# A hybrid decoder layer on one core: SBUF tiles filled up to multiples of 256 bytes, and attention's PSUM banks divided three and three

## The chip, the core and the metric

One core of a Trainium2 chip runs the whole layer as one program. The metric is the device time of one execution in microseconds (us), lower is better. Most executions of a kernel agree closely, but the three timed ones of the kernel before spread over 15 us. TensorE (PE) multiplies matrices, VectorE (DVE), ScalarE (ACT) and GpSimd (POOL) do the rest, SyncE (SP) issues most DMAs. SBUF is the on-chip working memory of 128 partitions, and PSUM, with eight banks of 2 KB in each partition, takes TensorE's results.

## The reference

A decoder layer over 1024 tokens of width 1024, all in float32:

```
h = x
proj = rmsnorm(h) @ w_in                      # queries, keys, values, gates of two groups of heads
o_nsa = gated sum of three attention branches # 8 heads: compressed, selected blocks, window of 512
o_fox = softmax attention with cumulative log-forget bias   # 8 heads
h = h + concat(rmsnorm(o_nsa), rmsnorm(o_fox)) @ w_out
u = rmsnorm(h)
h = h + hierarchical mixture of experts(u)    # 4 groups x 4 experts, top group, top 2 in it
h = h + sigmoid(rmsnorm(h) @ w_ple_gate + b) * (p @ w_ple_proj)
return rmsnorm(h)
```

An expert is `silu(u @ w_gate) * (u @ w_up) @ w_down` with an inner width of 512.

## The kernel before

The program is five stages, one behind the other, with a barrier of all engines between them where a `Scope` ends: projection (`stage_project`), attention (`stage_attention`), output mix (`stage_mix`), experts (`stage_moe`) and the final stage (`stage_finish`).

**Matmuls in three parts.** For nearly full float32 precision each wide product is made of three matmuls (`mm3`, lines 140 to 142): ScalarE rounds an operand to a "hi" tile (fp32r), VectorE or GpSimd takes the remainder into a "lo" tile, and TensorE adds hi x hi, hi x lo and lo x hi in PSUM. In the page's names a matmul reads "out<-streamed,stationary": the stationary tile (128 x 128) is loaded as weights (PEld), the streamed one passes with up to 512 columns. Projection streams `prj_hT` against `att_w_hi`/`att_w_lo`; the mix streams `mix_w` against `mix_mT`; the experts stream `exp_g_hi`/`exp_g_lo` (gate and up weights) against `moe_xT`, and `exp_d_hi`/`exp_d_lo` against `moe_hT`; the final stage streams the same `exp_g` tiles (with other weights in them) against `fin_vT`.

**Experts.** Tokens are sorted into tiles of 128 by expert, 21 tiles here for 16 experts. A tile takes 16 x 3 matmuls for gate and up (`gate_up`), 8 transposes of the next tile's tokens, 8 x 3 matmuls for the tile before (`down`) and 4 transposes. Where a tile begins a new expert, ScalarE (L2006, L2012) and VectorE (L2097, L2102) split its 12 chunks of weights, and SyncE loads the chunks of the expert behind it as soon as the raw buffers are read.

**Attention.** `units` are (head, branch, half of the queries): 64 of them, cut into 240 `banks`, each up to 512 score columns. TensorE's loop over banks b is, in this order: the scores of bank b+1 (L1334, L1347), some minima of the next head (`minimum`, L1303), the causal masks of bank b+1 (L1356), now and then the transposition of a head's minima (`turn`, L1313), and the weighing of bank b's values by its probabilities (`weigh`, L1374). ScalarE makes the exponentials (L1426). The scores are in two PSUM banks (`ps_s`, `ST`). Minima go through a ring of `MX` = 4 banks (`ps_m`): `place` counts the bank, `ring_before` names what must have been read before TensorE writes it, the minimum taken by VectorE (L1468, L1471; `min_taken`) or the rows copied by ScalarE (`min_copied`). The weighed sums of a unit go to one of two banks of `ps_o`: before the first weighing of unit u TensorE waits for `o_made` of unit u-2. VectorE's order is: the minima of bank b, then, if a unit has ended, its `leave` (L1495, L1499, L1502, L1506 or L1511), which divides the sums and signals `o_made` (behind L1511 by a semaphore instruction of its own, L1515). The blocks branch has one bank to a unit, the others three to seven.

The memory map of the program before has 16,512 bytes taken ahead of the kernel's first tile `all_c`, whose address is thus 16,512. The addresses of the tiles that the text speaks of, modulo 256:

| tiles | start modulo 256 |
|---|---|
| all_c (address 16,512) | 128 |
| att_o (address 25,856), att_cos, att_sin, att_w_out, att_w_raw, att_w_hi, att_w_lo, att_q_two0 | 0 |
| prj_hT_hi, prj_hT_lo | 128 |
| att_k_raw0, att_q_raw1, att_q_one1 and 2, att_q_two1 and 2, att_k_one1, att_k_two1, att_w_one1, att_w_two, att_x_one, att_x_two, att_prob, tok_kc_hi, tok_kc_lo | 192 |
| mix_w_hi, mix_w_lo | 0 |
| mix_mT_hi, mix_mT_lo, mix_x, mix_h, mix_u | 128 |
| exp_g_raw, exp_d_raw, exp_g_hi, exp_g_lo, exp_d_hi, exp_d_lo, exp_h | 0 |
| moe_xT_hi, moe_xT_lo, moe_hT_hi, moe_hT_lo, moe_y | 64 |
| fin_vT_hi, fin_vT_lo | 0 |

A 128-column slice is 512 bytes, so slices start at the same place modulo 256 as their tile. In attention the first buffer of several sets is a part of the projection's weight tiles (`held`): `att_w_hi` in a score row is q_one of every third head (or k_two), `att_w_lo` is k_one or w_one of the first group.

Of the kernel before, what the change touches and what calls it, by code (L numbers as in the profile page):

```python
# [29 lines left out]
F32 = mybir.dt.float32  # L30
F32R = mybir.dt.float32r
BF16 = mybir.dt.bfloat16
# [6 lines left out]
P = 128  # L39
# [41 lines left out]
HV = HD + 1  # L81
# [41 lines left out]
class Tally:  # L123

    def __init__(self, sem, base=0):
        self.sem, self.base, self.n = sem, base, 0
# [23 lines left out]

class Scope:

    def __init__(self, nc, name):
        self.nc, self.name, self.ctx, self.sems = nc, name, ExitStack(), []

    def __enter__(self):
        self.ctx.__enter__()
# [2 lines left out]
    def __exit__(self, *a):  # L162
        if self.sems:

            self.nc.all_engine_barrier()
            self.nc.clear_and_free_semaphores(self.sems)
            self.nc.all_engine_barrier()
        return self.ctx.__exit__(*a)

    def sb(self, name, shape, dt=F32):  # L170

        tile = self.ctx.enter_context(self.nc.sbuf_tensor(f"{self.name}_{name}", shape, dt))
        used = math.prod(shape[1:]) * (2 if dt is BF16 else 4)
        if 0 < used % 64 <= 32:
            self.ctx.enter_context(self.nc.sbuf_tensor(f"{self.name}_{name}_fill", [P, 8], F32))
        return tile

    def ps(self, name, shape, dt=F32):
        return self.ctx.enter_context(self.nc.psum_tensor(f"{self.name}_{name}", shape, dt))
# [8 lines left out]

def stage_project(nc, a, K, T):

# [7 lines left out]
    with Scope(nc, "prj") as sc:  # L198
# [5 lines left out]
        hT_lo = sc.sb("hT_lo", [P, KD, S], F32R)  # L204
        w_raw, w_hi, w_lo = (K[n] for n in ("w_raw", "w_hi", "w_lo"))

        k_raw0, q_raw0, q_one0, k_one0, k_two0, near0 = (t.rearrange("p k n -> p (k n)") for t in (
            w_raw[:, 0], w_raw[:, 1], w_hi[:, 1], w_lo[:, 1], w_hi[:, 0], w_lo[:, 0]))
        q_two0 = K["q_two0"][:]

        K["gf"] = K["o"][:, 4, 256:512].rearrange("p (t n) -> p t n", t=NT)
        K["kc_raw"] = K["o"][:, 4, 512:512 + GROUPS * P].rearrange("p (g n) -> p g n", g=GROUPS)
        mT0, mx0 = K["o"][0:3 * NT, 4, 768:768 + P].bitcast(F32R), K["o"][:, 4, 896:896 + NT * 5]

# [780 lines left out]
def stage_attention(nc, a, K, T):  # L995

    with Scope(nc, "att") as sc:
        HEADS = 2 * NH
        QS, RAW, ST, MX, PT, TM = 3, 2, 2, 4, 3, 2
        held = [K[n][:, s].rearrange("p k n -> p (k n)") for n in ("w_raw", "w_hi", "w_lo") for s in range(2)]  # L1000
        k_raw = [sc.sb("k_raw0", [P, S]), held[0]]
        q_raw = [held[1], sc.sb("q_raw1", [P, S])]
# [13 lines left out]
        tmp = sc.sb("tmp", [P, TM, 4, HD])  # L1016
        ps_s = sc.ps("ps_s", [P, ST, 512])
        ps_m = sc.ps("ps_m", [P, MX, 512])
        ps_o = sc.ps("ps_o", [P, 2, 512])

        q_in, k_in = [T["q_in0"], sc.sem("q_in1")], [T["k_in0"], T["k_in1"]]
        gk_hi, gk_lo, q_hi, q_lo, row_set, min_scored, min_taken, joined, min_turned, min_copied = (
# [18 lines left out]
        def pieces(b):  # L1041

            u, n = banks[b]
            out, at = [], 0
            for kb, qa, qb in BANKS[units[u][1]][units[u][2]][n]:
                out.append((kb, qa, qb, at))
                at += (qb - qa) * P
            return out, at
# [60 lines left out]
        with sc.block() as block:  # L1109
# [155 lines left out]
            def _(pe):  # L1265
                ident = c[:, K_ID:K_ID + P]

                def operands(i, br):

                    g, s = i // (NH // GROUPS), i % QS  # L1270
                    if br == CAUSAL:
                        return k_one[g], k_two[g], lambda kb: K["vsw"][:, kb, g, :]
                    if br == NEAR:
                        return w_one[g], w_two[g], lambda kb: K["vsw"][:, kb, GROUPS + g, :]
                    if br == BLOCKS:
                        return K["kc_hi"][:, g, :], K["kc_lo"][:, g, :], lambda kb: K["vc"][:, g, :]
                    f = i - NH
                    return fox_keys[f % QS][0], fox_keys[f % QS][1], lambda kb: K["vb"][:, kb, f, :]
# [82 lines left out]
                def weigh(b):  # L1361
                    u = banks[b][0]
                    i, br, half = units[u]
                    value = operands(i, br)[2]
                    first_of_unit = b == 0 or banks[b - 1][0] != u
                    pe.wait_ge(expd, b + 1)
                    if first_of_unit and u >= 2:
                        pe.wait_ge(o_made, u - 1)
                    first, final = first_of_unit, unit_end[u] == b + 1
                    parts = pieces(b)[0]  # L1370
                    for kb, qa, qb, at in parts:
                        for q in range(qa, qb):
                            end = final and (kb, q) == (parts[-1][0], qb - 1)
                            last = nc.tensor.matmul(ps_o[:, u % 2, (q % 4) * HV:(q % 4 + 1) * HV],  # L1374
                                                    prob[:, b % PT, at + (q - qa) * P:at + (q - qa + 1) * P], value(kb),
                                                    start=first, stop=end, skip_group_check=True)
                            first = False
                    last.then_inc(weighed, 1)
# [70 lines left out]
            def _(dve):  # L1449
# [38 lines left out]
                def leave(u):  # L1488
                    nonlocal parts
                    i, br, half = units[u]  # L1490
                    p = ps_o[:, u % 2, 0:4 * HV].rearrange("p (q d) -> p q d", q=4)
                    w = wt[:, u % 2, :]
                    qs = slice(4 * half, 4 * half + 4)
                    dve.wait_ge(weighed, unit_end[u])
                    own.inc(nc.vector.reciprocal(w, p[:, :, HD]))  # L1495
                    own.wait(dve)
                    if i < NH:
                        gate = i * 3 + (1 if br == CAUSAL else 2 if br == NEAR else 0)
                        own.inc(nc.vector.tensor_tensor(w, w, K["gate"][:, qs, gate], ALU.mult))  # L1499
                        own.wait(dve)  # L1500
                    if br == BLOCKS and half == 0:
                        own.inc(nc.vector.tensor_tensor(w[:, 0:1], w[:, 0:1], c[:, K_VALID:K_VALID + 1], ALU.mult))  # L1502
                        own.wait(dve)
                    wide = w.unsqueeze(2).to_broadcast((P, 4, HD))
                    if br in (CAUSAL, FOX):
                        nc.vector.tensor_tensor(K["o"][:, qs, i * HD:(i + 1) * HD], p[:, :, 0:HD], wide,  # L1506
                                                ALU.mult).then_inc(o_made, 1)
                        return
                    if parts >= TM:
                        dve.wait_ge(added, parts - TM + 1)  # L1510
                    own.inc(nc.vector.tensor_tensor(tmp[:, parts % TM], p[:, :, 0:HD], wide, ALU.mult))  # L1511
                    parts += 1
                    own.wait(dve)
                    dve.sem_inc(o_part, 1)
                    dve.sem_inc(o_made, 1)  # L1515

                first_keys(1, w_one[0], w_two[0])
                for b in range(NB):
# [4 lines left out]
                    if b and banks[b - 1][0] != banks[b][0]:  # L1523
                        leave(banks[b - 1][0])
                leave(banks[NB - 1][0])

# [1160 lines left out]
def build(nc, a, out):  # L2688
# [5 lines left out]
        "y": nc.dram_tensor("y_rows", [TILES * P, D], F32).ap(),  # L2694
    }
    K = {}
    with Scope(nc, "all") as outer:

        T["stored"] = [outer.sem(f"stored{i}") for i in range(2)]
# [58 lines left out]
```

## Time and profile before

| | us |
|---|---|
| median of the three timed executions | 1461.89 |
| the three | 1464.17, 1461.89, 1449.14 |
| the profiled execution, its own time | 1452.9 |
| its span in the trace | 1451.2 |
| its mean granted TensorE clock | 0.965 |

The profiled execution's own time is its span and 1.7 us around it. Stages by the trace, roughly: projection to 313, attention 314 to 714, mix to 853, routing and experts to 1300, final stage to 1451. TensorE's listed durations overlap, since matmuls are pipelined: the pace is read from starts.

### The profile page before, as it was taken

The page shows a single profiled execution, that of the slowest core. Times are in us where ns is not written, and L with a number is a line of the kernel's source. Part 1 is how long each engine was busy: PE and PEld are TensorE (multiplying, and loading weights), DVE is VectorE, ACT ScalarE, POOL GpSimd, SP SyncE. Part 2 cuts the span into 40 slices and gives each one's busy share as a digit, 9 for nine tenths or more (in the row PEclk, how much of TensorE's full clock was granted, in tenths as well). Part 3 has the DMA queues.
Part 4 walks back from the last instruction along what each step waited for, and adds up shares of the span by engine and source line. Part 5 has one row for each costly group of instructions (what it writes and reads, how often), then busy time and mean ns, then how long its engine had stood idle before and what let it go on. Part 6 is the DMA issues. An engine that isn't in the chain of part 4 may idle for free. (4 is left out here: it accounts for less than half of the span.)

```text
span 1451.2 us, 23331 instructions
## 1 busy us (share of the span) xinstructions
PE 1351.5 (93%) x7609; PEld 1133.5 (78%) x7610; DVE 773.9 (53%) x1575; ACT 619.8 (43%) x938; POOL 192.2 (13%) x219
## 2 busy tenths in 40 slices
PE   5899999989999999999889986999999999948996
PEld 4688888988888888888778864788888888837775
DVE  5734112646555554445353336678655767846762
ACT  5312111224333334444542213578644767845542
POOL 2100000115222123343000000000000000001100
PEclk9999999989999999999999977999999999969999
DMA  7233332122100111553232219699976979784411
GB/s 262 75 111 84 102 92 87 43 72 50 24 23 23 38 45 46 133 124 69 66 112 88 94 51 356 238 345 411 358 260 246 351 314 348 312 313 143 164 69 44
DMA packets 110994, 224.37 MB, mean 155 GB/s; under 512 B 17469, under 2 KB 44461, under 8 KB 110910
## 3 DMA queue, kind: packets, MB, share of 16 engines
q1 hardware_dynamic: 96694, 180.90, 36.7%
q0 software_dynamic: 10272, 30.57, 5.9%
q10 hardware_dynamic: 3944, 11.81, 2.2%
q8 instruction: 49, 0.80, 0.2%
q14 instruction: 35, 0.29, 0.1%
HBM read 178.66 MB, written 36.24 MB: 148 GB/s over the span
## 5 line engine op out<-in xcount | busy, mean ns | idle before, releaser
L1426 ACT ACTIVATE att_prob<-att_ps_s 128x512 f32<-128x512 f32 (+1 forms) x240 | 134.5, 561 | 240.0 <-PE att_ps_s L1356 200.0
L1471 DVE CUSTOM_DVE_ANT_0 att_ps_m<-att_ps_m,tok_maskb 128x128 f32<-128x128 f32 (+3 forms) x260 | 111.0, 474 | 140.7 <-PE att_ps_m L1303 137.7
L2097 DVE TENSOR_TENSOR exp_g_lo<-exp_g_raw,exp_g_hi 128x1024 fp32r<-128x1024 f32 x128 | 146.8, 1220 | 12.8 <-ACT exp_g_hi L2006 12.8
L1374 PE MATMUL att_ps_o<-tok_vsw,att_prob 128*128 128x65 f32 x1056 | 142.4, 277 | 0.8 <-DVEq L1515 0.5
L140 PE MATMUL moe_ps_g<-exp_g_hi,moe_xT_hi 128*128 128x512 f32 x336 | 136.2, 405 | 3.9 <-DVE exp_g_lo L2097 2.5
L1374 PEld LDWEIGHTS att_ps_o<-tok_vsw,att_prob 128*128 128x128 f32 x1056 | 134.5, 196 | 3.8 <-ACT att_prob L1426 1.0
L141 PE MATMUL moe_ps_g<-exp_g_lo,moe_xT_hi 128*128 128x512 f32 x336 | 134.4, 400 | 0.0
L142 PE MATMUL moe_ps_g<-exp_g_hi,moe_xT_lo 128*128 128x512 f32 x336 | 134.0, 399 | 0.0
L2006 ACT ACTIVATE exp_g_hi<-exp_g_raw 128x1024 fp32r<-128x1024 f32 x128 | 123.6, 1046 | 22.2 <-issue 11.5
L140 PE MATMUL prj_ps_w<-prj_hT_hi,att_w_hi 128*128 128x512 f32 x256 | 103.9, 406 | 5.4 <-ACT att_w_hi L492 2.1
L141 PE MATMUL prj_ps_w<-prj_hT_lo,att_w_hi 128*128 128x512 f32 x256 | 102.8, 402 | 0.0
L142 PE MATMUL prj_ps_w<-prj_hT_hi,att_w_lo 128*128 128x512 f32 x256 | 102.6, 401 | 0.0
L2102 DVE TENSOR_TENSOR exp_d_lo<-exp_d_raw,exp_d_hi 128x1024 fp32r<-128x1024 f32 x60 | 69.5, 1220 | 21.3 <-ACT exp_d_hi L2012 21.3
L140 PEld LDWEIGHTS moe_ps_g<-exp_g_hi,moe_xT_hi 128*128 128x128 f32 x336 | 64.1, 191 | 19.5 <-DVE exp_g_lo L2097 2.8
L142 PEld LDWEIGHTS moe_ps_g<-exp_g_hi,moe_xT_lo 128*128 128x128 f32 x336 | 64.1, 191 | 16.0
L1374 PE MATMUL att_ps_o<-tok_vb,att_prob 128*128 128x65 f32 x576 | 75.9, 273 | 0.0
L141 PEld LDWEIGHTS moe_ps_g<-exp_g_lo,moe_xT_hi 128*128 128x128 f32 x336 | 64.0, 191 | 14.8
L1374 PEld LDWEIGHTS att_ps_o<-tok_vb,att_prob 128*128 128x128 f32 x576 | 72.1, 192 | 3.5 <-ACT att_prob L1426 1.5
L140 PE MATMUL moe_ps_y<-exp_d_hi,moe_hT_hi 128*128 128x512 f32 x168 | 68.9, 410 | 5.1 <-DVE exp_d_lo L2102 5.1
L500 ACT ACTIVATE att_w_out<-prj_ps_w 128x512 f32<-128x512 f32 x28 | 16.7, 597 | 127.8 <-PE prj_ps_w L142 127.8
L141 PE MATMUL moe_ps_y<-exp_d_lo,moe_hT_hi 128*128 128x512 f32 x168 | 67.2, 400 | 0.0
L142 PE MATMUL moe_ps_y<-exp_d_hi,moe_hT_lo 128*128 128x512 f32 x168 | 67.1, 399 | 0.0
(468 smaller groups left out, 2908.1 us busy)
## 6 DMA issues: line engine op xcount, KB each, us to landing
exp_g_raw<-in_w_gate_e SPq DMA_DIRECT2D x128, 256.0 KB, 5.1
exp_g_raw<-in_w_up_e SPq DMA_DIRECT2D x128, 256.0 KB, 5.9
exp_d_raw<-in_w_down_e SPq DMA_DIRECT2D x64, 512.0 KB, 7.7
y_rows<-moe_y ACTq DMA_DIRECT2D x21, 512.0 KB, 6.1
att_w_raw<-in_w_in SPq DMA_DIRECT2D x16, 512.0 KB, 3.7
att_w_raw<-feat SPq DMA_DIRECT2D x30, 256.0 KB, 5.1
feat<-att_w_out POOLq DMA_DIRECT2D x14, 512.0 KB, 2.9
y_rows<-moe_zeros SPq DMA_DIRECT2D x10, 512.0 KB, 10.9
```

The lines of the kernel that those rows point to most:

```text
L140: nc.tensor.matmul(out, a_hi, b_hi, start=first, stop=False)
L141: nc.tensor.matmul(out, a_hi, b_lo, start=False, stop=False)
L142: return nc.tensor.matmul(out, a_lo, b_hi, start=False, stop=last)
L500: nc.scalar.activation(feat[:, s, h * 512:(h + 1) * 512], ps_w[:, h, :], ACT.Copy, scale=scale).then_inc(evac, 1)
L1374: last = nc.tensor.matmul(ps_o[:, u % 2, (q % 4) * HV:(q % 4 + 1) * HV], prob[:, b % PT, at + (q - qa) * P:at + (q - qa + 1) * P], value(k ...
L1426: nc.scalar.activation(prob[:, b % PT, 0:w], ps_s[:, b % ST, 0:w], ACT.Exp, scale=-1.0).then_inc(expd, 1)
L1471: last = nc.vector.tensor_tensor_reduce(p[:, at:at + w], p[:, at:at + w], K["maskb"][:, mask_at:mask_at + w], 1.0, -2.0 * NEG, ALU.add, AL ...
L2006: nc.scalar.activation(g_hi[:, ch % GR], g_raw[:, ch], ACT.Copy).then_inc(s_ghi, 1)
L2097: nc.vector.tensor_tensor(g_lo[:, ch % GR], g_raw[:, ch], g_hi[:, ch % GR].bitcast(F32), ALU.subtract).then_inc(s_glo, 1)
L2102: nc.vector.tensor_tensor(d_lo[:, ch % DR], raw[:, ch], d_hi[:, ch % DR].bitcast(F32), ALU.subtract).then_inc(s_dlo, 1)
```

## The change

`Scope` keeps a count `taken` of the bytes that tiles have taken, from 0 at the program's start, back to its old value where a scope ends. A tile of 1024 bytes or more gets a fill ahead of it that brings the count to a multiple of 256; the old 32-byte fills are gone. In attention `MX` goes from 4 to 3 and `ps_o` from two banks to `OB` = 3; the wait ahead of a unit's first weighing is for unit u-3, and three places that had `u % 2` for the bank have `u % OB`.

```diff
 class Scope:
+    taken, ROW = 0, 256
     def __init__(self, nc, name):
-        self.nc, self.name, self.ctx, self.sems = nc, name, ExitStack(), []
+        self.nc, self.name, self.ctx, self.sems, self.base = nc, name, ExitStack(), [], Scope.taken
     def __exit__(self, *a):
...
+        Scope.taken = self.base
         return self.ctx.__exit__(*a)
     def sb(self, name, shape, dt=F32):
-
-        tile = self.ctx.enter_context(self.nc.sbuf_tensor(f"{self.name}_{name}", shape, dt))
-        used = math.prod(shape[1:]) * (2 if dt is BF16 else 4)
-        if 0 < used % 64 <= 32:
-            self.ctx.enter_context(self.nc.sbuf_tensor(f"{self.name}_{name}_fill", [P, 8], F32))
-        return tile
+        size = -(-math.prod(shape[1:]) * (2 if dt is BF16 else 4) // 32) * 32
+        fill = -Scope.taken % self.ROW if size >= 1024 else 0
+        if fill:
+            self.ctx.enter_context(self.nc.sbuf_tensor(f"{self.name}_{name}_fill", [P, fill // 4], F32))
+        Scope.taken += fill + size
+        return self.ctx.enter_context(self.nc.sbuf_tensor(f"{self.name}_{name}", shape, dt))
...
-        QS, RAW, ST, MX, PT, TM = 3, 2, 2, 4, 3, 2
+        QS, RAW, ST, MX, PT, TM, OB = 3, 2, 2, 3, 3, 2, 3
...
-        ps_o = sc.ps("ps_o", [P, 2, 512])
+        ps_o = sc.ps("ps_o", [P, OB, 512])
...
-                    if first_of_unit and u >= 2:
-                        pe.wait_ge(o_made, u - 1)
+                    if first_of_unit and u >= OB:
+                        pe.wait_ge(o_made, u - OB + 1)
...
-                            last = nc.tensor.matmul(ps_o[:, u % 2, (q % 4) * HV:(q % 4 + 1) * HV],
+                            last = nc.tensor.matmul(ps_o[:, u % OB, (q % 4) * HV:(q % 4 + 1) * HV],
...
-                    p = ps_o[:, u % 2, 0:4 * HV].rearrange("p (q d) -> p q d", q=4)
+                    p = ps_o[:, u % OB, 0:4 * HV].rearrange("p (q d) -> p q d", q=4)
...
     K = {}
+    Scope.taken = 0
     with Scope(nc, "all") as outer:
```

## Rows read from the trace of the kernel before

**Rows 1.** The page: busy us, share, instructions; GB/s in 40 slices.
```profile
PE 1351.5 (93%) x7609; PEld 1133.5 (78%) x7610; DVE 773.9 (53%) x1575; ACT 619.8 (43%) x938; POOL 192.2 (13%) x219
GB/s 262 75 111 84 102 92 87 43 72 50 24 23 23 38 45 46 133 124 69 66 112 88 94 51 356 238 345 411 358 260 246 351 314 348 312 313 143 164 69 44
```
**Rows 2.** TensorE's waits, us, times, longest: attention (314 to 714), then experts (900 to 1256).
```profile
PE att_ps_o L1374 <- DVEq L1515: 4.7, 9, 0.6
...
PE moe_ps_g L140 <- DVE exp_g_lo L2097: 2.5, 1, 2.5
```
**Rows 3.** Timeline of TensorE in the experts: start us, us, what; nine matmuls stand between.
```profile
1022.79 0.40 PE L142 MATMUL moe_ps_g<-exp_g_hi,moe_xT_lo 128*128 128x512 f32 x1
...
1025.12 0.39 PE L140 MATMUL moe_ps_g<-exp_g_hi,moe_xT_hi 128*128 128x512 f32 x1
```
**Rows 4.** The same in the projection; nine matmuls stand between.
```profile
149.62 0.40 PE L140 MATMUL prj_ps_w<-prj_hT_hi,att_w_hi 128*128 128x512 f32 x1
...
151.95 0.39 PE L141 MATMUL prj_ps_w<-prj_hT_lo,att_w_hi 128*128 128x512 f32 x1
```
**Rows 5.** The same in the mix; seven matmuls stand between.
```profile
766.79 0.40 PE L140 MATMUL mix_ps_y<-mix_w_hi,mix_mT_hi 128*128 128x512 f32 x1
...
768.65 0.40 PE L142 MATMUL mix_ps_y<-mix_w_hi,mix_mT_lo 128*128 128x512 f32 x1
```
**Rows 6.** The same in the final stage; nine matmuls stand between.
```profile
1380.73 0.39 PE L140 MATMUL fin_ps_g<-exp_g_hi,fin_vT_hi 128*128 128x512 f32 x1
...
1382.99 0.39 PE L141 MATMUL fin_ps_g<-exp_g_lo,fin_vT_hi 128*128 128x512 f32 x1
```
**Rows 7.** Groups of TensorE by form, 340 to 714: count, busy us, mean ns of one.
```profile
L1334 PE MATMUL att_ps_s<-att_q_one,att_k_one 128*128 128x512 f32 x30 | 14.3, 477 | 0.0
...
L1334 PE MATMUL att_ps_s<-att_w_hi,att_w_lo 128*128 128x512 f32 x10 | 4.8, 479 | 0.0
...
L1334 PE MATMUL att_ps_s<-att_w_hi,att_w_one 128*128 128x512 f32 x3 | 1.4, 482 | 0.0
```
**Rows 8.** Groups over the whole span; L141 and L142 have L140's counts.
```profile
L140 PE MATMUL moe_ps_g<-exp_g_hi,moe_xT_hi 128*128 128x512 f32 x336 | 136.2, 405 | 3.9 <-DVE exp_g_lo L2097 2.5 <-DVE moe_xT_lo L2120 1.4
L140 PE MATMUL prj_ps_w<-prj_hT_hi,att_w_hi 128*128 128x512 f32 x256 | 103.9, 406 | 5.4 <-ACT att_w_hi L492 2.1 <-ACT att_w_hi L485 1.7 <-DVE prj_hT_lo L607 1.6
L140 PE MATMUL moe_ps_y<-exp_d_hi,moe_hT_hi 128*128 128x512 f32 x168 | 68.9, 410 | 5.1 <-DVE exp_d_lo L2102 5.1
L140 PE MATMUL mix_ps_y<-mix_w_hi,mix_mT_hi 128*128 128x512 f32 x128 | 53.5, 418 | 1.6 <-DVE mix_mT_lo L1681 1.5
```
**Rows 9.** Timeline of TensorE: the first gate matmul of two tiles of tokens.
```profile
1020.83 0.48 PE L140 MATMUL moe_ps_g<-exp_g_hi,moe_xT_hi 128*128 128x512 f32 x1
...
1038.94 0.48 PE L140 MATMUL moe_ps_g<-exp_g_hi,moe_xT_hi 128*128 128x512 f32 x1
```
**Rows 10.** Window 1200 to 1260: busy us of PE, PEld, DVE, ACT, POOL, clock, DMA share, GB/s.
```profile
1200.00:1260.00 60.00, 60.00 (x280) 48.78 (x279) 49.75 (x50) 45.79 (x54) 3.43 (x6) 1.00 0.97 374
```
**Rows 11.** ScalarE's waits, 890 to 1310: the one on a load of experts' weights.
```profile
ACT exp_d_hi L2012 <- DMA exp_d_raw<-in_w_down_e: 0.3, 1, 0.3
```
**Rows 12.** DMA issues: count, KB each, median us from issue to landing.
```profile
att_w_out<-in_w_out SPq DMA_DIRECT2D x8, 512.0 KB, 4.5
mix_x<-in_x SPq DMA_DIRECT2D x8, 512.0 KB, 4.6
```
**Rows 13.** Timeline around a unit's first weighing: TensorE, then VectorE.
```profile
455.39 0.23 PE L1356 MATMUL att_ps_s<-tok_identb,tok_maskb 128*128 128x128 bf16 x1
456.22 1.08 PE L1374 MATMUL att_ps_o<-tok_vc,att_prob 128*128 128x65 f32 x8 [0.60 <-DVEq L1515]
...
455.50 0.42 DVE L1511 TENSOR_TENSOR att_tmp<-att_ps_o,att_wt 128x256 f32<-128x256 f32 x1
```
**Rows 14.** Timeline where the ring of minima is tightest.
```profile
329.93 0.14 DVE L1471 DVE_READ_ACCUMULATOR2_ANT att_mx<- 128x1 f32 x1
...
330.25 0.68 PE L1303 MATMUL att_ps_m<-att_w_lo,att_q_one 128*128 128x512 f32 x2
```

## The prediction

> **What bounds the kernel now.** I read the page's busy rows first. The reader is to see one full engine: TensorE is busy for 93% of the span and nothing else passes 53% [rows 1]. The chain that ended last holds only the last stage, so it does not rank the stages. I then read TensorE's waits in attention and in the experts [rows 2]: the largest that recurs is 4.7 us of idle in 400 us of attention, and the experts' largest is 2.5 us once, in 356 us. So the time is the sum of TensorE's instructions, and the question is how far apart they start. A matmul's listed duration overlaps its successor's, so I read starts in the timeline. Ten steps of 512-column matmuls take 2.33 us in the experts [rows 3], 2.33 us in the projection [rows 4], eight take 1.86 us in the output mix [rows 5], and ten take 2.26 us in the final stage [rows 6]. That is 0.233, 0.233, 0.2325 and 0.226 us per matmul, at the full clock.
>
> The final stage streams the very tiles that the experts stream (exp_g_hi, exp_g_lo); only the stationary tile differs. By the memory map told above, final: both tiles start at a multiple of 256 bytes. Experts: stationary 64 past, streamed 0. Mix: stationary 128, streamed 0. Projection: stationary 0, streamed 128. So every stage whose two tiles start differently modulo 256 runs 0.0065 to 0.007 us per matmul slower than the one where they start alike. The steps within each stretch are even (0.22 to 0.24), so it is a pace and not a few stalls.
>
> **Part one, the start of the tiles.** Scope counts from 0, but the first tile of the program starts at byte 16,512, which is 64 times 256 plus 128. all_c is rounded to 7,904 bytes, the fill then brings `taken` to a multiple of 256, and the true address is 16,512 more. So after the change each tile of 1 KB or more stands 128 past a multiple of 256, none at a multiple (att_o goes from 25,856 to 25,984). Taken as absolute alignment, the change does the opposite of what it says; taken as alignment of tiles to each other, it does all of it: 128 against 128 in each of the four stages. The fills grow the map by under 1 KB, and no instruction is added.
>
> Which of the two counts? Attention has all four mixtures, in pairs of matmuls only [rows 7]. Score matmuls with both tiles at 192 take 477 ns, with both at 0 479, with 0 against 192 482 (three of them). The differences are small, since no long run of equal matmuls stands there, but "both off" is no slower than "both on", and the dearest is mixed. That speaks for relative alignment. I take it.
>
> The sum under it, per matmul 0.0067 us (between the 0.0065 and 0.007 above):
> - Experts: 3 x 336 + 3 x 168 = 1512 matmuls [rows 8], 10.1 us. One tile of tokens holds 72 and now takes 18.11 us, from start to start [rows 9]; 72 x 0.233 + 12 transposes of 0.11 is 18.1, so nothing else is in it. It should come to 17.6.
> - Projection: 3 x 256 = 768, 5.1 us; 4.5 taken, since its first ones run at the low clock or wait.
> - Mix: 3 x 128 = 384, 2.6 us; 2.1 taken for the same reason.
> - Final stage: stays at 0.226, 0.
> - Attention's wide scores and minima, some 400 in short bursts: bound 0 and 400 x 0.0067 = 2.7 us; I take 0.5, nearest to the 2 to 5 ns between those of [rows 7].
> Together 17.2 us; the bounds are 0 (or worse, below) and 20.5.
>
> What is late next in the experts? VectorE makes 12 remainders of 1.22 us each for a new expert, some 85% of a tile's time in the densest stretch, and the DMA engines are busy 97% there at 374 GB/s [rows 10]. ScalarE's splits wait for a load of experts' weights once, for 0.3 us [rows 11], and a chunk is loaded one expert ahead. 2.8% less time for the same bytes asks 385 GB/s, below the 411 of the busiest slice [rows 1]. I cost that at 0; if the cover were gone it would give back at most the experts' 10.1.
>
> The loads' target moves from 0 to 128 past 256. The loads of mix_x (target at 128) land in 4.6 us and those of the w_out ring (target at 0) in 4.5, both 512 KB [rows 12]. The Trainium skill, "DMA: Bandwidth & Descriptors", section "How a descriptor splits into AXI transactions", says that a descriptor that doesn't start at a multiple of 256 bytes pays for the bytes back to that boundary; by it a 2 KB row at 128 would cost 68 beats for 64, an estimate of 6% from that page, on the 97% stretch. The 0.1 us between the two loads hardly shows it, and no trace here has weights loaded off a multiple of 256. It is one reason why the adverse chance below is not smaller.
>
> The same skill, "SBUF — State Buffer", section "A bandwidth-pool intuition that's wrong (but worth ruling out)", gives weight loads a read port independent of the streamed operand's. By it no start address would matter to TensorE and part one would be worth 0. The experts and the final stage [rows 3, 6] disagree, with 0.233 against 0.226 for the same streamed tiles.
>
> **Part two, three banks for the sums.** Before a unit's first weighing, TensorE waits until VectorE has emptied the unit before the last. In [rows 13] the mask matmul starts at 455.39, the first weighing at 456.22, 0.83 us later, right behind the multiply of 455.50 and its semaphore. Without the wait the step is no longer than the mask matmul's listed 0.23, so 0.6 (the idle in the row) to 0.8 us are lost, because VectorE takes a minimum ahead of that multiply. The waits give nine such, 4.7 us of idle [rows 2]; idle starts only after the modelled end of the mask matmul (0.23 us), so each of the nine costs more than its idle time: 4.7 + 9 x 0.2 = 6.5. With three banks the wait is for the unit one earlier, emptied at least a whole bank (some 2 us) before. What could be late next is ScalarE's exponential of that bank; behind it no wait as large stands in attention's list. Bounds 4.7 and 6.5; I take 6.0.
>
> **Part three, three banks for the ring.** TensorE writes minimum m after VectorE has read m-3 instead of m-4. Behind that wait would stand the mask matmul, the turn and the weighing, and ScalarE's exponential would wait for them. The tightest place is in head 0's banks [rows 14]: the second of the two minima that start at 330.25 (0.3 us later, 330.55) would need the bank that VectorE left at 329.93 + 0.14 = 330.07, where with four banks it needs the one before. So 0.4 to 0.5 us remain. In the whole of attention TensorE's waits have no row for a minimum [rows 2]. Cost 0; each of nine stalls that goes takes up to 0.8 us of cover away, so 0.4 may be missing behind it, at most 9 x 0.4 = 3.6 us. Below nothing it can't be, a bank fewer frees no work.
>
> **Sum.** 17.2 + 6.0 = 23.2 us less than the profiled execution's 1452.9: 1429.7. The three timed runs have a median of 1461.9, 9.0 higher, and scatter by 15. With the profiled run they are two near 1450 and two near 1463; their middle is 1457.4, and from it I get 1434.
>
> **Rivals.**
> - Alignment doesn't reach the pace, or both off is like one off. Then projection, mix and experts keep 0.233, and the final stage's 3 x (128 + 24) = 456 matmuls lose 0.007 each, +3.2. With part two's -6.0 that is -2.8: 1454.6. For: the weak signal in attention. Against: the same streamed tiles at two paces. The Trainium skill's rule of separate read ports, cited above, is on this rival's side.
> - Adverse: absolute starts count, and each of two tiles off a 256 boundary adds 0.007. Then 2664 matmuls go from 0.233 to 0.240, +18.6, and 456 from 0.226 to 0.240, +6.4; less 6.0 is +19: 1476. It decides from the first long run of the projection on. For: one tile off costs the same whether it is streamed or stationary [rows 4, 5], as a sum of two surcharges would have it. Against: both at 192 in attention is not dearer.
> - The pace comes, but the ring of three takes what the sums' third bank gave: 1457.4 - 17.2 = 1440.
>
> **Chances.** The forecast 0.50; pace without part two 0.07; no pace 0.30; adverse 0.13. About 1% is what a measurement here can tell from no change. The first two (0.57) are faster by more, but for 0.01 that scatter may bring under it; so faster 0.56, same 0.31, slower 0.13. The range goes from 1424 (the bounds 20.5 and 6.5, and a few us of scatter) to 1462, which takes in the rival without pace with its scatter and leaves the adverse one out. The likeliest case's own range is 1424 to 1445.
>
> **What would show it.** Ten steps of expert matmuls in 2.26 us and a tile in 17.6 (right); 2.33 and 18.11 (no pace); 2.40 and 18.6 (adverse). The final stage tells as much: 2.26 kept, 2.33 or 2.40. TensorE's waits in attention without the nine behind VectorE's semaphore, and none of L1303's matmuls behind VectorE in their place. Waits of the experts' splits for weight loads would prove the cover wrong.

## The result, and the profile after

The changed kernel takes 1434.8 us (median of four executions, 1433.7 to 1440.8), the kernel before 1462.9 in the four beside it: ratio 0.985, 95% interval 0.9805 to 0.9895. The forecast was 1434. The profiled executions are 1452.9 and 1433.8 us, 19.1 apart, where the sum of the prediction had 23.2. The executions of one kernel scatter by some 15 us with the clock that TensorE was granted; 45 executions of the kernel before, taken with the experiments below, have a median of 1455.0. The table at equal clock, at the end of the experiments, puts the two facts together.

The page after. Columns are busy us, share and instructions, then the clock in 40 slices:

```profile
PE 1336.2 (93%) x7609; PEld 1132.2 (79%) x7610; DVE 773.8 (54%) x1575; ACT 620.7 (43%) x938; POOL 192.3 (13%) x219
...
PEclk9999999989999999999989978999999999979998
```

The instructions are the same ones [rows 1]; TensorE is busy for 15.3 us less and is still the one full engine.

The timeline of TensorE, in the order experts, projection, mix, final stage (start us, us, what). Nine matmuls stand between the two of a pair, seven in the mix:

```profile
1008.97 0.39 PE L140 MATMUL moe_ps_g<-exp_g_hi,moe_xT_hi 128*128 128x512 f32 x1
...
1011.24 0.39 PE L141 MATMUL moe_ps_g<-exp_g_lo,moe_xT_hi 128*128 128x512 f32 x1
...
147.12 0.39 PE L142 MATMUL prj_ps_w<-prj_hT_hi,att_w_lo 128*128 128x512 f32 x1
...
149.39 0.39 PE L140 MATMUL prj_ps_w<-prj_hT_hi,att_w_hi 128*128 128x512 f32 x1
...
765.50 0.39 PE L140 MATMUL mix_ps_y<-mix_w_hi,mix_mT_hi 128*128 128x512 f32 x1
...
767.33 0.39 PE L142 MATMUL mix_ps_y<-mix_w_hi,mix_mT_lo 128*128 128x512 f32 x1
...
1361.10 0.39 PE L141 MATMUL fin_ps_g<-exp_g_lo,fin_vT_hi 128*128 128x512 f32 x1
...
1363.37 0.39 PE L142 MATMUL fin_ps_g<-exp_g_hi,fin_vT_lo 128*128 128x512 f32 x1
```

Ten steps take 2.27 us in the experts and in the projection, where they took 2.33 [rows 3, 4]; eight take 1.83 in the mix after 1.86 [rows 5]; the final stage stays, 2.27 after 2.26 [rows 6]. A tile of tokens goes from first gate matmul to first gate matmul in 17.69 us, after 18.11 [rows 9]:

```profile
1006.14 0.48 PE L140 MATMUL moe_ps_g<-exp_g_hi,moe_xT_hi 128*128 128x512 f32 x1
...
1023.83 0.48 PE L140 MATMUL moe_ps_g<-exp_g_hi,moe_xT_hi 128*128 128x512 f32 x1
```

TensorE's waits in attention, 308 to 712 (what was waited for: us in total, times, longest):

```profile
PE att_ps_s L1337 <- PEq L169: 4.1, 1, 4.1
PE mix_ps_l L1790 <- PEq L169: 1.9, 1, 1.9
PE att_ps_o L1377 <- ACT att_prob L1429: 0.3, 1, 0.3
```

The nine waits behind VectorE's semaphore [rows 2] are gone and none of the minima (L1306) has come. The same two matmuls as in [rows 13], the mask and then the first weighing of the unit, now read:

```profile
449.67 0.23 PE L1359 MATMUL att_ps_s<-tok_identb,tok_maskb 128*128 128x128 bf16 x1
449.73 1.06 PE L1377 MATMUL att_ps_o<-tok_vc,att_prob 128*128 128x65 f32 x8
```

0.07 us from start to start (0.06 by the rounded rows), where it was 0.83.

Both traces hold the same 7609 matmuls in the same order, so the step from each to the next can be compared one by one. That splits the 19.1 us:

| from start to start of the matmuls | us less | steps |
| --- | --- | --- |
| long products at the high clock in both: experts | 8.55 | 1458 |
| the same, projection | 4.26 | 740 |
| the same, mix | 1.66 | 346 |
| the same, attention and final stage | -0.13 | 674 |
| first weighings of a unit, attention | 6.38 | 10 |
| steps in which one trace is at half clock and the other not, shorter products and all else | -1.6 | |

The last row is a balance of large parts. Attention begins with a stretch at half clock in both, which costs some 3 us more in the later trace, while the projection lost some 3 less. In the final stage less half clock gives back some 1.4 us, and two waits of TensorE at its start, one of them new, take 1.4 away.

### The profile page after: what moved, and what is told of

It is laid out like the page before. It is cut to its first block and busy times, and to the rows that moved or that the text cites. A ratio compares the mean times of both kernels' runs of the same rounds, so it can differ in the third digit from the quotient of the medians.

```text
span 1432.1 us, 23330 instructions
## 1 busy us (share of the span) xinstructions
PE 1336.2 (93%) x7609; PEld 1132.2 (79%) x7610; DVE 773.8 (54%) x1575; ACT 620.7 (43%) x938; POOL 192.3 (13%) x219
## 5 line engine op out<-in xcount | busy, mean ns | idle before, releaser
L2100 DVE TENSOR_TENSOR exp_g_lo<-exp_g_raw,exp_g_hi 128x1024 fp32r<-128x1024 f32 x128 | 146.9, 1221 | 10.1 <-ACT exp_g_hi L2009 10.1
L140 PE MATMUL moe_ps_g<-exp_g_hi,moe_xT_hi 128*128 128x512 f32 x336 | 134.5, 400 | 4.0 <-DVE exp_g_lo L2100 2.5
L2009 ACT ACTIVATE exp_g_hi<-exp_g_raw 128x1024 fp32r<-128x1024 f32 x128 | 123.6, 1048 | 20.8 <-issue 10.7
L141 PE MATMUL moe_ps_g<-exp_g_lo,moe_xT_hi 128*128 128x512 f32 x336 | 132.6, 394 | 0.0
L142 PE MATMUL moe_ps_g<-exp_g_hi,moe_xT_lo 128*128 128x512 f32 x336 | 132.5, 394 | 0.0
L140 PE MATMUL prj_ps_w<-prj_hT_hi,att_w_hi 128*128 128x512 f32 x256 | 102.0, 399 | 5.7 <-issue 2.5
L141 PE MATMUL prj_ps_w<-prj_hT_lo,att_w_hi 128*128 128x512 f32 x256 | 101.1, 395 | 0.0
L142 PE MATMUL prj_ps_w<-prj_hT_hi,att_w_lo 128*128 128x512 f32 x256 | 100.9, 394 | 0.0
L140 PEld LDWEIGHTS moe_ps_g<-exp_g_hi,moe_xT_hi 128*128 128x128 f32 x336 | 64.1, 191 | 17.5 <-DVE exp_g_lo L2100 2.8
L142 PEld LDWEIGHTS moe_ps_g<-exp_g_hi,moe_xT_lo 128*128 128x128 f32 x336 | 64.1, 191 | 13.7
L141 PEld LDWEIGHTS moe_ps_g<-exp_g_lo,moe_xT_hi 128*128 128x128 f32 x336 | 64.2, 191 | 12.9
L140 PE MATMUL moe_ps_y<-exp_d_hi,moe_hT_hi 128*128 128x512 f32 x168 | 68.2, 406 | 5.2 <-DVE exp_d_lo L2105 5.2
L2015 ACT ACTIVATE exp_d_hi<-exp_d_raw 128x1024 fp32r<-128x1024 f32 x60 | 59.3, 1050 | 24.7 <-issue 14.3
L142 PE MATMUL moe_ps_y<-exp_d_hi,moe_hT_lo 128*128 128x512 f32 x168 | 66.4, 395 | 0.0
```

The source lines that it names most:

```text
L140: nc.tensor.matmul(out, a_hi, b_hi, start=first, stop=False)
L141: nc.tensor.matmul(out, a_hi, b_lo, start=False, stop=False)
L142: return nc.tensor.matmul(out, a_lo, b_hi, start=False, stop=last)
L2009: nc.scalar.activation(g_hi[:, ch % GR], g_raw[:, ch], ACT.Copy).then_inc(s_ghi, 1)
L2015: nc.scalar.activation(d_hi[:, ch % DR], raw[:, ch], ACT.Copy).then_inc(s_dhi, 1)
L2100: nc.vector.tensor_tensor(g_lo[:, ch % GR], g_raw[:, ch], g_hi[:, ch % GR].bitcast(F32), ALU.subtract).then_inc(s_glo, 1)
```

## The experiments

In all of them the diff is against the changed kernel, except in the second. A tile's start is its address in the map modulo 256, and a distance is the start of the stationary tile minus that of the streamed one.

**1. The tiles alone.**

```
-        QS, RAW, ST, MX, PT, TM, OB = 3, 2, 2, 3, 3, 2, 3
+        QS, RAW, ST, MX, PT, TM, OB = 3, 2, 2, 4, 3, 2, 2
```

Expected: 

> The changed kernel's tile starts, with attention's banks as before (two for the sums, four for the ring). Theory 'starts of two tiles to each other': experts, projection and mix keep the pace of the changed kernel, 0.227 us between starts of 512-column matmuls, and the ten waits for the sums' banks come back, 6.4 us in all: 1434.8 + 6.4 = 1441. Rival 'the ring of three costs something too': the waits come back and less than 6.4 is lost, 1435 to 1439, since four banks in the ring give part of it back. Rival 'the banks gave more than the waits show': 1443 and above.

Measured: 1443.6 us median of ten (1438.2 to 1455.1). By this number alone it would be the last rival; at equal clock (the table below) it is 1441.8, 6.9 above the changed kernel, where the first theory has 6.4. The pace is the changed kernel's, and in its waits the old row is back:

```profile
PE att_ps_o L1377 <- DVEq L1518: 4.6, 9, 0.6
```

Against the changed kernel's first profile its first weighings cost 6.32 us in ten steps, and its long steps differ by 0.14 us in all. The first theory holds by the trace. The profiled times differ by only 4.4, since this execution drew a better clock (0.968 after 0.965).

**2. The banks alone,** in the kernel before, whose tiles stay where they were.

```
-        QS, RAW, ST, MX, PT, TM = 3, 2, 2, 4, 3, 2
+        QS, RAW, ST, MX, PT, TM, OB = 3, 2, 2, 3, 3, 2, 3
...
-                    if first_of_unit and u >= 2:
-                        pe.wait_ge(o_made, u - 1)
+                    if first_of_unit and u >= OB:
+                        pe.wait_ge(o_made, u - OB + 1)
```

Expected: 

> The kernel before with three banks for the sums and three for the ring, and its tiles where they were. Theory: pace stays at 0.233 in the three stages, the ten waits are gone, 6.4 us: 1462.9 - 6.4 = 1456.5 by medians, 1452.9 - 6.4 = 1446.5 against the profiled execution. Rival 'the ring of three costs something': a gain of 0 to 4 us. Together with e1_align_only the two parts should add up to the whole change's 28 us of medians or 19.2 us of profiles; if each alone is far from its share, the parts lean on each other.

Measured: 1446.9 median of ten, not the 1456.5 expected of medians, since the base of that, 1462.9, was high. The profiled execution is 1446.9 against the 1446.5 expected. The pace is 0.233 as before, and the waits of attention are

```profile
PE att_ps_s L1334 <- PEq L167: 4.1, 1, 4.1
PE mix_ps_l L1787 <- PEq L167: 1.9, 1, 1.9
PE mix_ps_x L1728 <- DVE att_o L1675: 0.3, 1, 0.3
PE att_ps_o L1374 <- ACT att_prob L1426: 0.3, 1, 0.3
```

The first weighings are 6.17 us shorter. The parts don't lean on each other: 6.2 here, 14.5 of pace in the first experiment.

**3. True multiples of 256.** The changed kernel puts its tiles 128 past one. Here they stand at 0:

```
-    Scope.taken = 0
+    Scope.taken = 128
```

Expected: 

> The changed kernel with every tile of 1 KB or more at a true multiple of 256 bytes instead of 128 past one. Theory 'to each other': nothing changes, 1434.8 with a pace of 0.227 in all four stages. Rival 'absolute starts count as well': each tile off the line costs something that both kernels still pay, and with 3120 long matmuls the time falls, by 9 us for each 0.003 us; pace 0.224 or less, 1426 or less. Rival 'loads of weights pay for a target 128 past a line': the loads' packets of 4096 bytes get shorter than in the changed kernel; TensorE is the bound, so the time stays.

Measured: 1439.3 median of four, the profiled one 1431.1. The long steps of this trace and of the changed kernel's are the same to 0.2 us over all 3200 of them. So it makes no difference whether both tiles stand at 0 or both at 128, and the adverse rival, that each of two tiles off the line costs its own surcharge, fails from the other side as well.

The rival on the loads was right as well. In the experts (900 to 1240 us, 11,400 to 11,900 packets of 4096 bytes in each trace) the median packet takes 159 ns whatever the target. With targets at 0 hardly one takes longer (1 to 2%), and the mean is 161.9 to 162.6 ns in the four traces of that kind. With targets 128 past, about half take longer (46 to 50%, the upper tenth 169 ns or more), and the mean is 164.9 to 165.6 in the ten others. The packets of 2048 bytes, the row for which the prediction worked out 6%, show the same: means of 89.0 to 89.5 ns against 90.2 to 91.2. That is some 2% more time of a DMA engine for either. The rule of the Trainium skill cited in the prediction ("DMA: Bandwidth & Descriptors", "How a descriptor splits into AXI transactions") gives 132 beats for 128, 3%, for a packet of 4 KB, an estimate from that page. The rule has the right sign, and it overstates the 2 KB packets; nor would it leave half of the packets as they were. It costs nothing here, since no matmul waits for a load of weights.

**4. Five distances at once.** One tile of each long product is moved off the other again, by five amounts, and nothing else.

```
+    PAST = {f"{n}_{part}": past for n, past in (("prj_hT", 32), ("mix_mT", 96), ("moe_xT", 64), ("moe_hT", 128), ("fin_vT", 192)) for part in ("hi", "lo")}
...
-        fill = -Scope.taken % self.ROW if size >= 1024 else 0
+        fill = (self.PAST.get(f"{self.name}_{name}", 0) - Scope.taken) % self.ROW if size >= 1024 else 0
```

Expected: 

> The changed kernel with one of the two tiles of each long product moved away from the other modulo 256: projection by 32 bytes (streamed side), mix by 96, gate and up by 64, down by 128, final stage by 192 (these four on the stationary side). Nothing else differs. Theory 'to each other': every one of them returns to 0.232 to 0.234 us between starts, the final stage for the first time: 3120 matmuls by 0.0058 = 18 us more, 1453. Rival 'only some distances cost': of the five paces some stay at 0.227. Rival 'it was not the distance but something else that moved with the map' (loads, other tiles' places): all stay at 0.227, 1435.

Measured: 1451.2 median of eight. The projection moved its streamed tile, so its distance is -32, or 224 modulo 256. The pace returns to 0.233 everywhere but in the final stage, 15.7 us in all; there the rival "only some distances cost" is nearer than the theory. That makes the distance a cause and not a companion: the rest of the map moved by 256 bytes at most, and kept its starts modulo 256, and only the distance within a product was changed. The final stage, at 192, rose by a quarter of that. Ten steps of the experts (distance 64), then of the final stage (192), here 2.33 and 2.29 us:

```profile
1044.69 0.39 PE L141 MATMUL moe_ps_g<-exp_g_lo,moe_xT_hi 128*128 128x512 f32 x1
...
1047.02 0.40 PE L142 MATMUL moe_ps_g<-exp_g_hi,moe_xT_lo 128*128 128x512 f32 x1
...
1393.27 0.39 PE L140 MATMUL fin_ps_g<-exp_g_hi,fin_vT_hi 128*128 128x512 f32 x1
...
1395.56 0.39 PE L141 MATMUL fin_ps_g<-exp_g_lo,fin_vT_hi 128*128 128x512 f32 x1
```

**5. The stage or the distance?** The distances are exchanged.

```
+    PAST = {f"{n}_{part}": past for n, past in (("prj_hT", 192), ("mix_mT", 192), ("moe_xT", 192), ("moe_hT", 32), ("fin_vT", 64)) for part in ("hi", "lo")}
```

Expected: 

> e4 gave 0.0057 to 0.0067 us more at 32, 96, 64 and 128, but only 0.0014 more in the final stage at 192. Here the distances are exchanged: projection 192 (streamed side), mix 192, gate and up 192, down 32, final stage 64. Theory 'the distance of 192 is cheap where the stationary tile is the one ahead': gate, up and mix at 0.228 to 0.230, final stage back at 0.233, down at 0.233. Rival 'the final stage is cheap whatever the distance', since its weights come in blocks of 24 and not of 16: final stage at 0.229 again, gate, up and mix at 0.233. For the projection, where the streamed tile is the one ahead, the first theory says 0.233, as stationary minus streamed is then 64.

Measured: 1440.4 us once. Now the experts take 2.29 and the final stage 2.33 for ten steps:

```profile
1051.15 0.39 PE L141 MATMUL moe_ps_g<-exp_g_lo,moe_xT_hi 128*128 128x512 f32 x1
...
1053.44 0.39 PE L142 MATMUL moe_ps_g<-exp_g_hi,moe_xT_lo 128*128 128x512 f32 x1
...
1387.60 0.39 PE L140 MATMUL fin_ps_g<-exp_g_hi,fin_vT_hi 128*128 128x512 f32 x1
...
1389.93 0.39 PE L141 MATMUL fin_ps_g<-exp_g_lo,fin_vT_hi 128*128 128x512 f32 x1
```

It is the distance. With the last one, 160, from the run below, and the distances of the kernel before, the mean step of all long products at the high clock is, in ns:

| distance | 0 | 32 | 64 | 96 | 128 | 160 | 192 | 224 |
| --- | --- | --- | --- | --- | --- | --- | --- | --- |
| projection | 226.9 | | 233.3 | | 232.6 | 233.4 | | 233.3 |
| mix | 227.6 | | | 234.2 | 232.7 | 233.3 | 229.2 | |
| gate and up | 227.2 | | 233.3 | | | | 229.3 | |
| down | 227.2 | 233.0 | 233.2 | | 233.1 | | | |
| final stage | 227.9 | | 233.3 | | | 233.4 | 229.3 | |

The means hold the steps at the start of each run of matmuls (mostly 24 to 96 of them), which are longer. In the down product they are 226.7 ns inside an unbroken run at distance 0, and 233.3 for gate and up at 64: at 2.4 GHz 544 and 560 cycles for 512 columns. At 192 they go 226, 229, 232 in turn.

**6. Whose meeting is it?** Only some halves are moved.

```
+    PAST = dict(exp_g_lo=64, moe_xT_lo=64, fin_vT_lo=64, moe_hT_lo=64, mix_mT_hi=64)
```

Expected: 

> Whose meeting is it? The changed kernel with the lower halves alone moved by 64 bytes: experts' streamed exp_g_lo and stationary moe_xT_lo, the final stage's stationary fin_vT_lo, the down product's stationary moe_hT_lo, and in the mix the upper stationary half mix_mT_hi. A product runs as (hi, hi), (hi stationary, lo streamed), (lo, hi). Theory 'own pair', a matmul is slow where its own stationary and streamed tiles start differently: in gate and up two of three are slow, 0.227 + 2/3 x 0.006 = 0.231 on the mean. Theory 'neighbour', it is slow where the tile that is streamed and the stationary tile that is loaded meanwhile for the next matmul start differently: there moe_xT_lo is loaded while exp_g_lo is streamed, both 64 further, so all three stay at 0.2267. Final stage, gate and up: the same two answers, 0.231 or 0.227. Down by either theory one of three, 0.229. Mix by either two of three, 0.231.

Measured, 1437.6 us once; mean step in ns: gate and up 231.1, final stage 231.2, down 230.9, mix 232.5. Gate and up rule the neighbour out, since the tile streamed and the tile to be loaded for the next matmul stood alike throughout. The first two fit "own pair" at 231, but down (229 expected) and mix (231) are 1.5 to 2 above.

**7. One tile of one product, and the distance 160.**

```
+    PAST = dict(moe_xT_lo=64, exp_d_lo=64, prj_hT_hi=96, prj_hT_lo=96, mix_mT_hi=160, mix_mT_lo=160, fin_vT_hi=160, fin_vT_lo=160)
```

Expected: 

> The rule 'own pair' of e5 is tried with one tile alone: in gate and up only the stationary moe_xT_lo moves by 64 (one product of three), in the down product only the streamed exp_d_lo (one of three). By that rule both means are 0.2267 + 1/3 x 0.0062 = 0.229; e5's down product with one stationary tile moved gave 0.231, so the rival is 0.231 in gate and up as well, and the rule per matmul would be wrong in its size. The last distance: stationary ahead of streamed by 160 in projection, mix and final stage. Theory 'only 192 is cheap': 0.233. Rival 'the price grows from 256 downwards' (224 gave 0.2333, so this is unlikely): 0.230 or 0.231.

Measured: 1449.8 us once. 160 costs the full price (table above). With one product of three at another distance, gate and up take 230.9 and down 231.7 ns, not 229. So one uneven product of three already costs some two thirds of what three cost. Told apart by their lines, inside unbroken runs, the step that begins with the uneven product takes 235.4 ns in gate and up and the two others 228.3 and 229.0; the down product of the run before, also with its stationary lo tile moved, has 235.0, 228.2 and 228.9. So the uneven product pays most, over 8 ns, and its neighbours some 2. With the streamed tile moved (down, here) the three are even, 231.3 to 232.3. "Own pair" as a surcharge per matmul is wrong in size; which accesses meet is open.

**8. The smaller ring alone,** with the bank it frees left unused: MX 3, OB 2.

Expected: 

> The changed kernel with three banks in the ring and only two for the sums, one bank left unused: the price of the smaller ring alone. Theory 'nothing waits for the ring': attention as in e1_align_only, the ten waits there with 6.3 us, no wait of a minimum for VectorE, start to end 398.7 us. Rival 'the ring of three costs a little': attention some 0.5 to 3 us longer than in e1_align_only at the same granted clock, with waits at the minima.

Measured: 1438.8 us once, attention from first to last matmul 398.8 us against 398.7 in the first experiment, the waits for the sums' banks back (4.6 us, 9 times), none at a minimum. The smaller ring costs nothing.

**9 and 10. A ring of two,** to see how near three was: MX 2, OB 3.

Expected of the first: 

> The changed kernel with two banks in the ring, to see whether the wait exists at all and how near three was to it. In the trace of the kernel after, a minimum starts 0.46 us at the least and 2.2 us at the median after VectorE has read the one three before. One bank less takes a minimum's period of some 0.7 to 2 us from that. Theory 'the ring is a matter of slack': attention gets waits of its minima (TensorE, the line of the minima, behind VectorE) and 5 to 60 us more. Rival 'the ring never binds': attention stays at 395 us.

Measured: 1441.1 us once, attention 404.3 us, 9.0 more than in the changed kernel and within the 5 to 60 expected. But the waits of the minima, which were to make them, are small:

```profile
PE att_ps_m L1306 <- DVE att_mx L1474: 0.5, 1, 0.5
PE att_ps_o L1377 <- ACT att_prob L1429: 0.3, 1, 0.3
PE att_ps_m L1306 <- DVE att_mx L1471: 0.3, 1, 0.3
```

Two steps are 0.74 and 0.45 us longer; 6.5 of the 9.0 us stand in steps at half clock. Windows of six us of this kernel (TensorE busy and its instructions, granted clock, share and GB/s of the DMA engines):

```profile
324.00:330.00 6.00, 5.46 (x21) 0.50 0.10 22
330.00:336.00 6.00, 6.00 (x26) 0.50 0.01 3
336.00:342.00 6.00, 6.00 (x32) 0.68 0.00 0
```

I could not tell from it whether the wait had kept the clock low, so it ran again. Expected: 

> The ring of two once more. In e8 attention was 9.0 us longer than in the changed kernel's first profile, but only some 1 to 3 us of it stood in waits; the rest was a stretch at the low clock that went on to 339 us, and e9, the changed kernel itself, had one to 341. Over all executions a kernel's time falls by 1.2 us for 0.001 of granted clock: the changed kernel stands at 1434.9 at 0.965. Theory 'a ring of two costs its waits only': 1436 to 1438 at 0.965, and some of the executions at 0.962 or above. Rival 'its wait keeps the clock low': every execution below 0.963, as in e8.

Measured: five executions, 1435.0 to 1438.1 at 0.965 to 0.968, attention 395.3 us in the profile, with the same two long steps (0.79 and 0.44 us) and the full clock from 320 us on. A ring of two costs its waits; the low clock of the first did not come again.

**11. The changed kernel again.**

Expected: 

> The changed kernel once more, many executions. In the runs so far a kernel's time follows the granted clock of the execution: the kernel before gave 1452 to 1455 at 0.964 to 0.968 and 1460 to 1465 at 0.958 to 0.960. The changed kernel was timed four times, none of them below 0.962. Theory 'the clock falls as often in both': of some ten executions two to four come out near 1444 to 1447 at 0.956 to 0.959, the others at 1431 to 1436, and at equal granted clock the changed kernel is 19 to 20 us faster. Rival 'the change also keeps the clock up': none of them falls.

Measured: ratio 0.9849, interval 0.9816 to 0.9882. Six executions, two of them at 1441.8 and 1444.6 with 0.959 and 0.958, so the change doesn't keep the clock up. The longest was the profiled one, and it shows where such an execution loses. In the first profile of the changed kernel attention begins so:

```profile
312.00:318.00 6.00, 6.00 (x26) 0.50 1.03 238
318.00:324.00 6.00, 6.00 (x24) 0.50 0.51 122
324.00:330.00 6.00, 6.00 (x40) 0.86 0.11 25
330.00:336.00 6.00, 6.00 (x48) 1.00 0.00 0
```

and in this one

```profile
318.00:324.00 6.00, 6.00 (x26) 0.50 0.72 158
324.00:330.00 6.00, 6.00 (x25) 0.50 0.36 87
330.00:336.00 6.00, 6.00 (x25) 0.50 0.01 3
336.00:342.00 6.00, 6.00 (x26) 0.54 0.00 0
```

The same program, with a busy TensorE, is at 1.2 GHz for some 15 us longer. In both, TensorE had stood idle for 4.1 us just before attention, at the barrier, and the half clock shows within a us of its first matmul there. Of the 10.7 us between the two traces, some 9 are steps at half clock in one and not in the other, 6 of them here.

**12. True multiples again.**

Expected: 

> The kernel of e3 once more beside the changed one, since its median of four was 4.5 us higher while its profile was 2.7 us shorter. Theory 'true multiples of 256 bring nothing beyond alike': at equal granted clock within 1 us of the changed kernel. Rival: 2 us faster or more at equal clock.

Measured: 1435.7 median of six, the changed kernel beside it 1436.7. No version here beats the changed kernel by more than the measurement can tell.

**The same clock for all.** The time falls by 1.2 us for each 0.001 of granted clock, fitted for every kernel with eight or more executions (1.0 to 1.3). Brought to 0.965 with that slope, the means are:

| kernel | executions | us at 0.965 | to before |
| --- | --- | --- | --- |
| before | 45 | 1455.1 | |
| banks alone | 10 | 1448.1 | -7.0 |
| tiles alone | 10 | 1441.8 | -13.3 |
| changed | 10 | 1434.9 | -20.2 |
| tiles at 0, banks as changed | 10 | 1434.4 | -20.7 |
| ring of two | 6 | 1437.6 | -17.5 |
| five distances | 8 | 1449.8 | -5.3 |

The standard errors are 0.2 to 0.6 us. 7.0 and 13.3 make 20.3: the two parts add. The runs come from three chips or more; the kernel before, timed beside them on each, stands at 1454.8 to 1455.6 at 0.965.

## Why the prediction was right, and by how much it was not

- *The pace.* Right in mechanism: 0.233 became 0.227 in the three stages and stayed in the fourth, with the tiles 128 past a multiple. The term was mis-sized: 17.2 forecast, 14.3 found. I took 0.0067 us per matmul, from ten steps of 2.26 against 2.33 us. Each of these readings is rounded, and the gain is not one number. Well inside an unbroken run the step shortens by 6.4 ns in gate and up and 6.8 in down, but by 5.9 in the projection and 5.6 in the mix, whose distance was 128. The steps that follow a run's start are long in both kernels and gain little. The mean over a whole stage is 5.9 in the experts, 5.8 in the projection and 4.8 in the mix; a tile of tokens gained 0.42 us where 0.5 was forecast. Experts 8.6 for 10.1, projection 4.3 for 4.5, mix 1.7 for 2.1, attention nothing for 0.5.
- *The reason for the pace.* I weighed two pictures, "both alike" and "each off costs". The runs hold the first, but only as far as the distance: 0 is free, 192 costs 2 ns, the others 6 to 7. The weak signal in attention [rows 7] pointed the right way; by itself, with three matmuls of the mixed form, it would not have carried the step without the final stage. That form was streamed 0 against stationary 192, by the table the cheapest of the uneven distances. The independent port for weights of the Trainium skill ("SBUF — State Buffer", the section cited in the prediction) was read in the prediction as saying that start addresses don't matter to TensorE. That reading falls here: 1455.1 against 1441.8 us with nothing but start addresses changed. Whether the two reads have ports of their own no run here shows.
- *The sums' banks.* 6.0 forecast, 6.4 found in ten first weighings (6.2 and 6.3 in the two runs that took one part alone). The waits view had nine and 4.7 us; adding the time that the modelled end of the mask matmul covers was needed. The step without the wait is 0.07 us, and not up to the 0.23 listed. ScalarE's exponential came next, as forecast, at no price.
- *The ring.* 0 forecast, 0 found with three banks. Even two cost only 2.7 us at equal clock, of which the two long steps show 1.2; where the rest lies was not traced. The 0.4 us left in [rows 14] was real cover.
- *The loads.* Costed at 0, and TensorE has the same rows of waits in the experts as before. The cover did get thinner: ScalarE's wait for a load of w_down, 0.3 us once in [rows 11], is now

```profile
ACT exp_d_hi L2015 <- DMA exp_d_raw<-in_w_down_e: 10.2, 6, 5.9
```

By the prediction's own sign, waits of the splits for weight loads, the cover was misjudged; no time was lost, because TensorE did not come to wait for these splits. The faster pace and the new start of the targets each bring such waits alone. In us, over 870 to 1310:

| ScalarE's wait for w_down | targets at 0 | targets 128 past |
| --- | --- | --- |
| old pace | 0.3 (before), 2.5 (banks alone) | 7.4 (five distances) |
| new pace | 7.1 and 6.5 (tiles at 0, two profiles) | 9.4 to 11.5 (six profiles with the changed kernel's tiles) |

A landing of w_down went from 7.7 us to 9.1, by the 48 of 64 whose landing each of the two traces shows. That the faster TensorE calls for the same bytes in less time, and that packets to a target 128 past are longer, fits both directions; how much of the waits each of these makes was not traced.

- *The sum and the median.* 23.2 forecast, 19.1 by the profiles, 20.2 at equal clock: 3 too many. The base was 1457.4, the middle of four executions, where 45 have 1455.1 at 0.965: 2.3 too high. The two cancel, and 1434 against 1434.8 flatters the working. The first medians, 28 us apart, flatter the change in the same way: three of the four executions of before lay above 1461, and the others of that kernel that were granted 0.957 to 0.961 took 1460.4 to 1465.5.

## What to carry to other kernels

Where TensorE is full and its matmuls are long, read the step from start to start in each stage, at the full clock, beside the map of the tiles: a stage that is 3% slower with the same shapes is a hint that its stationary and streamed tile may start differently modulo 256. Give both the same start; 0 and 128 did equally well here, others were not tried. And where the time of a kernel moves with the granted clock, compare at equal clock, or step by step between two traces with the same instructions, before a few microseconds are given to a cause.

## What was not expected of the hardware

- A distance of 192 bytes costs 2 ns of the 6.6, in three stages, and 64, which is as far the other way, the whole.
- One product of three at another distance costs two thirds of three (230.9 and 231.7 ns for 229 by share), and the matmuls beside it pay a part of it.
- The stretch at 1.2 GHz with which attention begins ended between 320 and 342 us in executions of nearly the same program, and at 326 and 342 in two of the same one, with TensorE busy throughout in both; it is some 6 of the 10.7 us between these two.
- A target 128 past a multiple of 256 lengthens half of the 4 KB packets, mostly by 1 to 13 ns from the 159 ns that nearly all take at a multiple, and their mean by 2%.
